# One weight unit loaded by transfers of 49, 49 and 30 partitions in place of one of 128

## What is computed

```python
for e in range(N_EXPERTS):                      # 8 experts, EXPERT_FF = 3584
    he = jax.nn.silu(t @ w1[e]) * (t @ w3[e])   # w1, w3: 1024 x 3584
    out = out + gates[:, e:e + 1].astype(t.dtype) * (he @ w2[e])   # w2: 3584 x 1024
```

## Time and profile before

| What | Value |
|---|---|
| median of three executions | 1211.14 us |
| the profiled execution | 1210.93 us |
| its span, first to last instruction | 1209.2 us |
| TensorE busy | 1168.0 us (97%) |
| VectorE, ScalarE, GpSimd busy | 348.9, 262.5, 58.5 us |
| read from HBM | 417.45 MB |
| granted TensorE clock | 0.999 |

### The profile page before, as it was taken

How to read it: one execution, slowest core, us unless ns; L and a number is a source line. 1 busy time by engine, 2 the same in 40 slices (tenths; PEclk the granted TensorE clock), 3 DMA queues, 4 the chain that set the end, 5 groups by cost and what they waited for, 6 DMA issues and landing times.

```text
span 1209.2 us, 24031 instructions
## 1 busy us (share of the span) xinstructions
PE 1168.0 (97%) x10764; PEld 654.5 (54%) x10765; DVE 348.9 (29%) x605; ACT 262.5 (22%) x396; POOL 58.5 (5%) x114
## 2 busy tenths in 40 slices
PE   8999999999999999999999999999998799999996
PEld 7888888888997444443334433344443234443331
DVE  6977776677995001001001100100100010010000
ACT  5785344335771000000000000000000000000000
POOL 5402300000001000000000000000000000000000
PEclk9999999999999999999999999999999999999999
DMA  7559655653159999999999999999999999999995
GB/s 245 184 175 318 209 197 180 203 178 136 61 192 423 418 406 361 391 427 425 426 424 426 425 427 424 426 426 423 426 426 424 428 424 426 425 426 424 426 426 233
DMA packets 72699, 419.25 MB, mean 347 GB/s; under 512 B 5331, under 2 KB 39760, under 8 KB 48145
## 3 DMA queue, kind: packets, MB, share of 16 engines
q1 hardware_dynamic: 70576, 414.21, 84.9%
q0 software_dynamic: 2016, 3.46, 0.8%
HBM read 417.45 MB, written 2.10 MB: 347 GB/s over the span
## 4 chain that ended last, share of the span: by engine, by line
PE 81%; DMA 14%; ACT 2%; DVE 2%; issue 1%; POOL 0%; SPq 0%; DVEq 0%; ACTq 0%
PE ps L1309 35%; PE ps L1391 15%; DMA w_ring<-in_moe_w_dram 13%; PE ps L1046 7%; PE ps L763 5%; PE ps L765 5%; PE ps L764 5%; PE ps L1051 3%; PE ps L1337 1%; ACT expert_h L1842 1%; PE ps L1324 0%; DMA residual<-in_x_dram 0%; PE ps L1292 0%; PE ps L1330 0%; PE ps L884 0%
## 5 line engine op out<-in xcount | busy, mean ns | idle before, releaser
L1309 PE MATMUL ps<-w_ring,expert_in 128*32 128x512 f32 (+1 forms) x5120 | 487.9, 540 | 11.7 <-DMA w_ring<-in_moe_w_dram 10.4
L1309 PEld LDWEIGHTS ps<-w_ring,expert_in 128*32 128x32 f32 x5120 | 186.4, 110 | 305.8 <-issue 284.0
L1391 PE MATMUL ps<-w_ring,expert_h 128*32 128x512 f32 (+1 forms) x2688 | 246.6, 522 | 13.2 <-DMA w_ring<-in_moe_w_dram 7.8
L1391 PEld LDWEIGHTS ps<-w_ring,expert_h 128*32 128x32 f32 x2688 | 90.6, 110 | 160.8 <-issue 129.4
L1886 DVE TENSOR_TENSOR w_lo<-w_raw,w_hi 128x2048 fp32r<-128x2048 f32 (+2 forms) x63 | 127.5, 2050 | 35.4 <-ACT w_hi L1460 35.3
L1046 PE MATMUL ps<-act_both,w_hi 128*128 128x512 f32 x352 | 122.5, 397 | 0.0
L1460 ACT ACTIVATE w_hi<-w_raw 128x2048 fp32r<-128x2048 f32 (+2 forms) x62 | 104.4, 1717 | 3.8 <-DMA w_raw<-in_mla_w_kvb_dram 2.0
L2470 DVE TENSOR_TENSOR expert_h<-expert_h,ps 128x896 f32<-128x896 f32 x20 | 21.8, 1088 | 279.3 <-PE ps L1309 279.3
L1051 PE MATMUL ps<-act_both,w_lo 128*128 128x256 f32 x352 | 91.4, 280 | 0.0
L2431 DVE COPY slot_gate<-ps 128x2 f32<-128x2 f32 x8 | 1.3, 159 | 255.5 <-PE ps L1277 255.5
L1842 ACT ACTIVATE expert_h<-ps 128x896 f32<-128x896 f32 x20 | 17.9, 917 | 260.1 <-PE ps L1324 260.1
(11 more groups left out here) (374 smaller groups left out, 1069.6 us busy)
## 6 DMA issues: line engine op xcount, KB each, us to landing
w_ring<-in_moe_w_dram SPq DMA_DIRECT2D x191, 1792.0 KB, 34.1
w_raw<-in_ffn_w_dram SPq DMA_DIRECT2D x33, 1024.0 KB, 5.5
w_raw<-in_lru_w_in_dram SPq DMA_DIRECT2D x8, 1024.0 KB, 5.2
w_raw<-in_mla_w_o_dram SPq DMA_DIRECT2D x4, 1024.0 KB, 4.8
w_raw<-in_lru_w_out_dram SPq DMA_DIRECT2D x4, 1024.0 KB, 4.8
w_raw<-in_mla_w_in_dram SPq DMA_DIRECT2D x8, 352.0 KB, 7.2
w_raw<-in_mla_w_qb_dram SPq DMA_DIRECT2D x4, 576.0 KB, 4.1
w_raw<-in_mla_w_kvb_dram SPq DMA_DIRECT2D x2, 1024.0 KB, 12.2
```

Of the source, the lines that this page charges most:

```text
L1309: ins = pe.matmul(ps[j * STRIP:(j + 1) * STRIP, 2 * g + b, 0:wide], in_x[:, c, k, g * STRIP:(g + 1) * STRIP], w[:, j * PART + at:j * PART ...
L1391: return pe.matmul(ps[j * STRIP:(j + 1) * STRIP, out_bank(n, block), 0:wide], hT[:, a:a + STRIP], w[:, c0:c0 + wide], start=strip == 0 and ...
```

## The change

Unit 168 (FEW_UNIT: the first w1 unit of the last expert) is loaded by three transfers, to partitions 0 to 48, 49 to 97 and 98 to 127, in place of one to all 128. All three add to the semaphore of its ring place, so the counts that the waits of this and later units of that place use are worked out from the number of transfers. The bytes, their place and the wait before the first transfer are the same.

```diff
+        FEW_UNIT, SEVENTHS = (E - 1) * N_BODY + M_W1, (0, 49, 98, P)
+
+        def transfers(g):
+
+            return len(SEVENTHS) - 1 if g == FEW_UNIT else 1
+
+        def ring_transfers(i, n):
+
+            return sum(transfers(g) for g in range(i, n, RING))
+
...
                 g = n * N_BODY + u
-                return g % RING, 16 * (g // RING + 1)
+                return g % RING, 16 * ring_transfers(g % RING, g + 1)
             i = u % RING
-            return i, 16 * (ring_loads(i, E * N_BODY) + u // RING + 1)
+            return i, 16 * (ring_transfers(i, E * N_BODY) + u // RING + 1)
...
-                    if static and n == E - 1 and u == N_BODY - 1:
+                    if static and n * N_BODY + u == FEW_UNIT:
+                        for p, q in zip(SEVENTHS, SEVENTHS[1:]):
+                            sp.dma_start(dst[p:q], src[p:q]).then_inc(ring_landed[slot], 16)
+                    elif static and n == E - 1 and u == N_BODY - 1:
                         for (lo, hi), piece in zip(LAST_PIECES, (ring_landed[slot], *last_landed)):
```

## The result

The change makes the kernel slower: 1231.74 us (1231.58 to 1231.96, four runs) against 1211.16 us, a ratio of 1.0168, 95% interval 1.0156 to 1.0181. That is 20.6 us more, where 3.2 us less were forecast and 4.3 us more was the worst rival.

The account below looks back on a forecast made before the run. The weight stream, ended by eight late DMA engines, was taken as the bound; -3.2 (late engines) + 0 (SP) + 0 (unit 168's wait) gave 1207.7 us profiled, 1207.9 us median, ratio 0.9973, range 1207.2 to 1215.8 us.

Parts of the forecast that it names:

- the worst rival: At the stream's end, loaded engines include a late one: 4.3 us more, 1215.4 us; chance 0.22.
- What bounds the kernel: Whole kernel: the weight stream's DMA engines set the end, eight late ones setting every landing; redistribution could bring 5.9 us at most.
- Rows per engine: Unit 168: seven engines carry 16 rows, eight carry 2, one none, against 8 each, at 0.534 us a row.
- Which engines: Stream's end: the seven loaded engines are the seven early ones, so the late eight are relieved and end 3.2 us sooner.
- the loaded seven are among the late eight: Rival at the stream's end: one late engine among the loaded makes the last landings 4.3 us later, 1215.4 us; chance 0.22.
- the relief is an illusion: Rival where rows are written: partitions get the same 8 rows, so the end stays, 1211.1 us; chance 0.25 including an even deal.
- SP: SP's queue: two more issues of 0.33 us each, bounds 0 and 5.5 us, hidden behind some 40 us of backlog: 0.
- Unit 168's own wait: TensorE's wait for unit 168's three landings: 9.8 us of room, hidden even if 4.3 us later: 0.
- no change: the release stays at 1195: Sign in the profile after for unchanged time: the DMA share's end and TensorE's last release stay at 1199 and 1195 us.
- slower: the release at 1199.3: Sign for slower: early engines end some 3 us sooner, the last 4 us later, TensorE's last release at 1199.3 us.
- wrong in another way: Signs in the profile after: a wait of L1309 for w_ring before 1142 us, or SP issues of many us after 1058.

Follow-up runs that it names:

- unit 96's run: The change's 49, 49 and 30 partitions applied to unit 96, the first of the fifth expert, in place of unit 168: 1226.11 us, ratio 1.0115.
- the probes: The kernel before with four tiny transfers of 7, 8, 15 and 16 partitions issued behind unit 191 on the same queue: 1210.87 us, ratio 0.9993.
- the quarter: Unit 168 in five transfers, every fourth partition from 0, 1 and 2, every eighth from 3 and 7, against the kernel before: 1215.74 us, ratio 1.0033.
- 64 and 64: Unit 168 in two transfers of 64 neighbouring partitions, 8 rows for each engine, against the kernel before: 1221.46 us, ratio 1.0085.
- 112 and 16: Unit 168 in transfers of 112 and 16 partitions, 8 rows for each engine, against the kernel before: 1225.06 us, ratio 1.0115.
- a step of 2: Unit 168 in two transfers of 64 partitions, the even and the odd ones, against the kernel before: 1210.8 us, ratio 0.9997.
- a step of 8: Unit 168 in eight transfers of 16 partitions, each taking every eighth one, against the kernel before: 1222.98 us, ratio 1.0094.
- three columns: Unit 168 in three transfers of 1195, 1195 and 1194 columns, each over all 128 partitions, against the kernel before: 1211.26 us, ratio 1.0007.

## Why the prediction was wrong

*What bounds the kernel: right.* The stream of weights sets the end, and a loss in it anywhere comes out at the end in full; unit 96's run shows this over 400 us.

*Rows per engine: right.* The 13 additional packets are those of 7 + 7 + 15 engines, hence 16, 2 and 0 rows.

*Which engines: wrong.* The step that failed is "the loaded seven are the early seven", chosen because both groups counted seven. Five of the seven are early and two late (the probes, and unit 169). A unit lands with its slowest engine, so the two late ones make the term +4.3 us and not -3.2. This was the rival *the loaded seven are among the late eight*, which I priced rightly and gave 0.22. That it takes one engine to make it true was in its text and not in its chance: with eight late engines of sixteen, a group of seven without a late one was the unlikely case.

*The writing side: the larger error, 16.4 us.* The rival *the relief is an illusion* had the right place and the wrong price. It argued that each group of partitions gets the same 8 rows, that a displaced row only takes the time that its usual engine is spared, and that the end stays. The step that failed is this conservation: while such rows are under way, the rate of all engines together falls to 204 to 250 of 425 GB/s (293 to 332 in the quarter), and what is missing is lost, not lent. Equal loads (64 and 64; 112 and 16) show it without the first error. So no upper bound of mine came from this mechanism: I had bounded a displaced row by its normal time, although no row of before showed a displaced one. And the loss comes in two bouts, one for the early and one for the late engines.

The Trainium skill (page DMA: Bandwidth & Descriptors, section The descriptor swizzle) gives the deal of 128: partitions 0 to 3 and 32 to 35 to the first engine, and so on, groups of four. The runs agree so far as they go: a step of 2 costs nothing (-0.4 us), the quarter with its steps of 4 and 8 little (4.4 us), a step of 8 and contiguous halves much (+11.8, +10.2 us). How a transfer of fewer rows is dealt out is not seen in any run. The Trainium skill (same page, section Rules for kernel authors) advises one transfer of 128 over two halves because the halves gain nothing. Here they cost 10.2 us.

*SP: right in substance.* The three columns show that three issues cost nothing. In the changed kernel SP is held up to 10.99 us by one issue; the share of busy DMA engines stays at 0.94 or more until 1200 us, so they didn't lack work for it.

*Unit 168's own wait: wrong, as a consequence.* I gave it 9.8 us of room. It landed about 21 us later, and TensorE idled 9.95 us. That idle isn't a cost of its own: the two parts of the table make up the whole loss without it.

*Which of my tests could have told.* The line "no change: the release stays at 1195" and the line "slower: the release at 1199.3" both missed. The two signs of "wrong in another way" came, a wait of L1309 (now L1322) before 1142 us and SP issues of many us, but I had tied no mechanism and no price to them; none of my pictures had a rate below 425 GB/s with all engines busy.

**What stays open.** Why all sixteen engines slow down and not only the pairs that meet. The runs show that the way in which the partitions are cut decides, that neither the load nor three transfers nor a shift of the rows read does, and that the total about halves. That the jam is where the rows are written is argued from these, and no run shows the place. Nor is the number of displaced rows a full measure: eight a piece cost 10.3 to 13.7 us.

## What to carry to other kernels

Load a full tile by one transfer over all 128 partitions, and if it must be cut, cut it by columns or by a step of two, so that, by the reading above, each row stays with the engine that usually brings it; in this stream, whose engines never paused, contiguous cuts of one unit in 192 cost 10 to 20 us. Look for it in the profile as a stretch with the DMA share at 1 and the GB/s at half. Before shifting load between engines, put tiny transfers of few partitions at the end of the queue: they cost nothing here, and tell how many of the engines that a small transfer uses are early.

## What was not expected of the hardware

A unit in contiguous pieces slows also the engines that are still at rows of the unit before: 222 to 230 GB/s of 425 with all sixteen busy, and nearly every row at about 1.03 us in place of 0.54. The engines of one stream, with equal shares, end it in two groups of eight, about 10 us apart (probes landing at 1187 to 1192 and at 1198.5 to 1200.8), and the groups don't follow the engines' order. Three transfers of columns and two of even and odd rows cost nothing, two of contiguous halves 10.2 us. After an idle of 9.95 us the granted clock of TensorE was 0.50 (1.2 GHz) in the window 1118 to 1120 us, and its first unit took 4.55 us in place of 3.21; the stream hid it.
